# A streaming encoder layer: two blocks of expert look-ups as one dense sweep, the other look-ups in one lane

## The reference

```
h   = x @ w_in                       # q, k, v of 8 forgetting heads (64 wide) and 4 differential heads (2x64), 8 gates
A   = softmax(q k^T / 8 + D[t] - D[s], causal) @ v          # D: running sum of log gates
B   = (softmax(q1 k1^T / 8 + bias) - lam * softmax(q2 k2^T / 8 + bias)) @ v    # chunk-causal, then RMS norm
x   = LayerNorm(alpha * x + concat(A, B) @ w_out)
q   = x @ w_pq                       # 8 heads x 2 halves x 128
s   = q . sub_keys                   # 128 keys in each half; top 16 of each; top 16 of the 256 sums
idx = i1 * 128 + i2                  # 8 x 16 = 128 experts of 16384 for each frame
g   = softmax(top sums)
y   = sum over the 128 of  g * gelu(x . u_tab[idx]) * v_tab[idx]
x   = LayerNorm(alpha * x + y)
```

## Time and profile before

| | us |
|---|---|
| median of three runs | 2214.57 |
| span of the profiled execution | 2113.0 |
| whole time of the profiled execution | not shown; the runs lie between 2211.59 and 2216.9 |
| PE, DVE, ACT, POOL busy | 1847.5, 1189.1, 694.1, 1293.6 |
| bytes moved by DMA | 759.05 MB, mean 359 GB/s |

### The profile page before, as it was taken

One profiled execution on the slowest core, in us unless ns is written; L12 is line 12 of the kernel. 1 busy time (PEld: TensorE's weight loads), 2 busy tenths in 40 slices (PEclk: granted clock), 3 DMA queues, 4 the chain that ended last, 5 costly groups with the idle time before them and its releaser, 6 DMA issues.

```text
span 2113.0 us, 25770 instructions
## 1 busy us (share of the span) xinstructions
PE 1847.5 (87%) x7056; PEld 1048.4 (50%) x7056; DVE 1189.1 (56%) x2936; ACT 694.1 (33%) x1925; POOL 1293.6 (61%) x1198
## 2 busy tenths in 40 slices
PE   6795999999879999998798999987999998986776
PEld 5564544446445444455464454553655554552332
DVE  2349444557864445478645354787434454797543
ACT  1301324632222246322222464222245663222221
POOL 2004774766667756666577566666446675667774
PEclk9897999999989999999899999999999999998989
DMA  9457999999999999999999999999979999999996
GB/s 344 170 183 287 408 408 383 339 360 399 404 347 399 408 391 330 360 392 399 345 400 408 392 328 360 390 400 347 368 287 353 373 398 387 345 366 344 396 408 264
DMA packets 213316, 759.05 MB, mean 359 GB/s; under 512 B 24400, under 2 KB 28792, under 8 KB 212904
## 3 DMA queue, kind: packets, MB, share of 16 engines
q0 software_dynamic: 167168, 612.07, 75.6%
q1 hardware_dynamic: 45992, 145.17, 18.1%
HBM read 747.14 MB, written 13.28 MB: 360 GB/s over the span
## 4 chain that ended last, share of the span: by engine, by line
PE 60%; DMA 17%; DVE 10%; issue 6%; ACT 4%; POOL 3%; DVEq 0%; POOLq 0%; ACTq 0%; SPq 0%; PEldq 0%
PE acc L629 34%; DMA vbuf<-in_peer_v,idx_cur 13%; PE ps_o L610 4%; PE ps_o L434 4%; DVE ubuf L1006 3%; PE ps_o L569 3%; PE ps_o L550 3%; PE ps_s L493 3%; DMA wring<-in_w_qk 2%; PE ps_t L513 2%; POOL ubuf L1049 2%; PE ps_o L461 2%; PE ps_s L497 1%; DMA ubuf<-in_peer_u,idx_cur 1%; ACT L675 1%
## 5 line engine op out<-in xcount | busy, mean ns | idle before, releaser
L629 PE MATMUL acc<-vbuf,diag 128*128 128x512 f32 x2304 | 1060.3, 612 | 118.1 <-DMA vbuf<-in_peer_v,idx_cur 98.6
L1049 POOL DMA_INDIRECT ubuf<-in_peer_u,idx_cur x576 | 663.3, 1152 | 394.7 <-DVE hid L1006 234.3
L629 PEld LDWEIGHTS acc<-vbuf,diag 128*128 128x128 f32 x2304 | 436.9, 196 | 673.0 <-issue 629.5
L1006 DVE CUSTOM_DVE_ANT_0 ubuf<-ubuf,x_cur 128x1024 f32<-128x1024 f32 x576 | 677.2, 1222 | 159.9 <-DMA ubuf<-in_peer_u,idx_cur 137.9
L1049 POOL DMA_INDIRECT vbuf<-in_peer_v,idx_cur x576 | 610.3, 1060 | 232.5 <-issue 154.1
L747 ACT ACTIVATE diag<-ident,coef 128x128 f32<-128x128 f32 x576 | 193.1, 392 | 153.8 <-PE acc L629 141.5
L434 PE MATMUL ps_o<-xT,wring 128*128 128x128 f32 x1280 | 170.9, 299 | 62.5 <-DMA wring<-in_w_qk 30.4
L434 PEld LDWEIGHTS ps_o<-xT,wring 128*128 128x128 f32 x1280 | 167.3, 214 | 76.8 <-issue 29.3
L832 DVE CUSTOM_DVE_ANT_0 region<-ps_s,region 128x512 f32<-128x512 f32 (+2 forms) x80 | 59.5, 744 | 235.8 <-PE ps_s L497 151.9
L610 PEld LDWEIGHTS ps_o<-region,wring 128*128 128x128 f32 x1280 | 151.3, 195 | 18.4 <-issue 16.6
L610 PE MATMUL ps_o<-region,wring 128*128 128x128 f32 x1280 | 152.7, 279 | 3.9 <-ACT region L710 3.9
(11 more groups left out here) (169 smaller groups left out, 1399.8 us busy)
## 6 DMA issues: line engine op xcount, KB each, us to landing
wring<-in_w_qk SPq DMA_DIRECT2D x80, 512.0 KB, 7.6
wring<-in_w_pq SPq DMA_DIRECT2D x80, 512.0 KB, 7.2
wring<-in_w_out SPq DMA_DIRECT2D x40, 512.0 KB, 7.2
wring<-in_w_v SPq DMA_DIRECT2D x20, 512.0 KB, 8.4
ubuf<-in_peer_u,idx_cur POOLq DMA_INDIRECT x576, 7.8
vbuf<-in_peer_v,idx_cur POOLq DMA_INDIRECT x576, 8.5
region<-scr_tpl SPq DMA_DIRECT2D x4, 1280.0 KB, 16.7
wring<-in_c_k SPq DMA_DIRECT2D x8, 512.0 KB, 7.4
```

Source lines behind the costliest of these rows:

```text
L629: last = pe.matmul(acc[:, hf * 512:(hf + 1) * 512], diag[:, j, :], vbuf[:, j, hf * 512:(hf + 1) * 512], start=first_slot, stop=last_slot)
L1006: nc.vector.tensor_tensor_reduce(out=ubuf[:, j, :], in0=ubuf[:, j, :], in1=x1_cur[:, :], scale=1.0, scalar=0.0, op0=ALU.mult, op1=ALU.add, ...
L1049: pool.indirect_dma_start(buf[:, j, :], None, a[table], bass.IndirectOffsetOnAxis(ap=idx_cur[:, at:at + 1], axis=0)).then_inc(landed_[j], 16)
```

## The change

Blocks 0 and 1 and the sample keep the gather form. Blocks 2 and 3 (256 frames) do without: a dense sweep reads both expert tables whole, 128 tiles of 128 experts. For each tile PE transposes the u tile (8 transposes), ACT copies it from PSUM, PE forms the hidden values of the 256 frames (8 matmuls with 256 columns), ACT applies Gelu, DVE multiplies with the gates of this tile, and for each four tiles PE forms the outputs (8 columns of frames' features x 4 tiles, 256 columns each), which DVE adds to `yT` in SBUF. The value part runs 24 tiles behind the hidden part.

The gates as a matrix (experts x frames) are made before: for each frame a matmul of two one-hot matrices, of the second and of the first key number, the latter scaled by the gate. POOL makes the one, DVE the other, ACT copies the result, and it is put into memory (`gate_spill`, 16 pieces of 1 MiB), from which chunks of 8 tiles are read back.

The lane of the slots (`j_`) has 320 slots: 128 of block 0, 128 of block 1, 64 of the sample, 333 steps. In a step POOL gathers u row j and v row j-9, and DVE does the dot product of slot j-3 and adds coefficient times row of slot j-12 to an accumulator in SBUF by a fused multiply and add. PE and the diagonal matrices have no part in it. The rings of rows hold four of each table.

The loop is gone: all five blocks are written out, and a function `weave` puts the steps of several lanes in one fixed order on every engine. In phase p stand beside each other: attention to queries of block p (28 steps), the projections of block p+1 (12 steps over the first 92%), the top-k of block p-1 (45 steps over the first 60%, now from a copy of the scores in SBUF), and a part of the slot lane (12 steps in phase 1, 28 in each of phases 2 to 4). Then come the gate build (64 steps) with 23 hidden steps and 20 slot steps, and the rest of the sweep (129 steps) with 217 slot steps and the sample's top-k over 5% to 40% of it.

Beside that: a prompt block takes only the keys up to its own end (128, 256, 384, 512), queries are used by halves of 64 partitions without padding, matmul results of four tiles are copied from PSUM at once, ACT instead of DVE scales most head outputs, the second norm's scale and shift are loaded spread over the partitions, the weight ring has seven places and none of the v tiles is held, and the last three norms stand at the end.

```diff
-            with pe.Fori(0, NBP - 1) as i:
-                for s, _ in enumerate(tensor_block(pe, i + 1, False)):
-                    if s >= 2:
-                        tensor_set(pe, i, s - 2)
...
+ORDER = (0, 1, 2, 3, NBP)
+SMP = ORDER.index(NBP)
+LAST = NB - 1
+DENSE = (2, 3)
+NT = len(DENSE) * P
+POS = {b: p for p, b in enumerate(ORDER)}
+WRING = 7
+X_STEPS, Y_STEPS, T_STEPS, I_STEPS = 12, 28, 45, 1
+G_STEPS = 32 * len(DENSE)
+TILES = NKEYS
+URING, VRING = 4, 8
+LAG = 24
+HRING = 30
+GTOK = 16
+TGS = NT // GTOK
+CHUNK = 8
+D_STEPS = TILES + LAG
+GRING = 4
+PARTS = ((0, POS[0]), (SLOTS, POS[1]), (2 * SLOTS, SMP))
+PSLOTS = 2 * SLOTS + DEC
+U_LAG, V_AT, V_LAG = 3, 9, 12
+J_STEPS = PSLOTS + V_LAG + 1
+J_CUTS = (0, 12, 40, 68, 96, 116, J_STEPS)
...
+X_SPAN = (0.0, 0.92)
+Y_SPAN = (0.0, 1.0)
+T_SPAN = (0.0, 0.6)
...
+        def mixers(p, y, x, t, i, j):
+            lanes = [(y(p), Y_STEPS) + Y_SPAN]
+            if p < LAST:
+                lanes.append((x(p + 1), X_STEPS) + X_SPAN)
+            if p:
+                lanes.append((t(p - 1), T_STEPS) + T_SPAN)
+                steps = range(J_CUTS[p - 1], J_CUTS[p])
+                lanes.append((j(steps), len(steps), 0.65 if p == 1 else 0.0, 1.0))
+            if p == LAST:
+                lanes.append((i(0), I_STEPS, 0.0, 0.01))
+            weave(*lanes)
+        def sweep(t, i, g, d, j):
+            weave((i(1), I_STEPS, 0.0, 1.0))
+            steps = range(J_CUTS[4], J_CUTS[5])
+            weave((g(), G_STEPS, 0.0, 1.0), (d(range(0, LAG - 1)), LAG - 1, 0.0, 1.0), (j(steps), len(steps), 0.0, 1.0))
+            steps = range(J_CUTS[5], J_CUTS[6])
+            weave((d(range(LAG - 1, D_STEPS)), D_STEPS - LAG + 1, 0.0, 1.0), (j(steps), len(steps), 0.0, 1.0),
+                  (t(LAST), T_STEPS, 0.05, 0.4))
...
+        def g_tensor(pe):
+            for n in range(G_STEPS):
+                pe.wait_ge(oh2_done, n + 1)
+                pe.wait_ge(oh1_done, n + 1)
+                if n == 0:
+                    pe.wait_ge(ids_out, len(DENSE))
+                if n >= 2:
+                    pe.wait_ge(gt_out, n - 1)
+                for j in range(4):
+                    last = pe.matmul(xb[:, n % 2, j * P:(j + 1) * P], oh2[n % 2][:, j, :], oh1[n % 2][:, j, :], start=True, stop=True)
+                last.then_inc(gt_done, 1)
+                yield
+        def d_tensor(pe, steps):
+            def turn(i):
+                pe.wait_ge(du_in[i % URING], 16 * (i // URING + 1))
+                for r in range(2):
+                    wait(pe, uT_out, 2 * i - 1 + r)
+                    for j in range(4):
+                        c = 4 * r + j
+                        last = pe.transpose(ps_s[:, c * P:(c + 1) * P], u_tile[i % URING][:, c * P:(c + 1) * P], ident[:, :])
+                    last.then_inc(uT_done, 1)
+            for i in steps:
+                if i == 0:
+                    pe.wait_ge(sc_out, 4 * NB)
+                    pe.wait_ge(qh_out, 4 * NB)
+                    pe.wait_ge(v_out, 2 * NB)
+                    turn(0)
+                if i + 1 < TILES:
+                    turn(i + 1)
+                if i < TILES:
+                    wait(pe, dg_done, i - 1)
+                    for c in range(KT):
+                        if c % 4 == 0:
+                            pe.wait_ge(uT_out, 2 * i + c // 4 + 1)
+                        last = pe.matmul(ps_o[:, i % 2, 0:NT], uT[i % 2][:, c, :], x1T[:, c, :], start=c == 0, stop=c == KT - 1)
+                    last.then_inc(dh_done, 1)
+                if i >= LAG:
+                    g, q = (i - LAG) // 4, (i - LAG) % 4
+                    if i == LAG:
+                        pe.wait_ge(gt_out, G_STEPS)
+                    if q == 0:
+                        pe.wait_ge(da_done, 4 * (g + 1))
+                        for j in range(4):
+                            v = 4 * g + j
+                            pe.wait_ge(dv_in[v % VRING], 16 * (v // VRING + 1))
+                    for dc in (2 * q, 2 * q + 1):
+                        n = KT * g + dc
+                        wait(pe, dy_out, n - 3)
+                        for j in range(4):
+                            e = 4 * g + j
+                            last = pe.matmul(y_banks[n % 4][:, 0:NT], v_tile[e % VRING][:, dc * P:(dc + 1) * P], hg[e % HRING],
+                                             start=j == 0, stop=j == 3)
+                        last.then_inc(dy_done, 1)
+                yield
...
+        def g_scalar(act):
+            for n in range(G_STEPS):
+                act.wait_ge(gt_done, n + 1)
+                tg = n // 4
+                if n % 4 == 0 and tg >= 2:
+                    act.wait_ge(spill[tg % 2], 16 * (tg // 2))
+                dst = gst[tg % 2][:, :, n % 4 * 4:n % 4 * 4 + 4].rearrange("p i t -> p t i")
+                nc.scalar.copy(dst, xb[:, n % 2, :].rearrange("p (t i) -> p t i", i=NKEYS)).then_inc(gt_out, 1)
+                yield
+        def d_scalar(act, steps):
+            def move(i):
+                if i >= 2:
+                    act.wait_ge(dh_done, i - 1)
+                for r in range(2):
+                    act.wait_ge(uT_done, 2 * i + r + 1)
+                    nc.scalar.copy(uT[i % 2][:, 4 * r:4 * r + 4, :],
+                                   ps_s[:, r * 512:(r + 1) * 512].rearrange("p (c e) -> p c e", e=P)).then_inc(uT_out, 1)
+            for i in steps:
+                if i == 0:
+                    act.wait_ge(out_k, 16 * NB)
+                    act.wait_ge(out_v, 16 * NB)
+                    move(0)
+                if i + 1 < TILES:
+                    move(i + 1)
+                if i < TILES:
+                    act.wait_ge(dh_done, i + 1)
+                    if i >= HRING:
+                        act.wait_ge(dy_done, KT * ((i - HRING) // 4 + 1))
+                    nc.scalar.activation(hg[i % HRING], ps_o[:, i % 2, 0:NT], ACT.Gelu).then_inc(dg_done, 1)
+                yield
...
+        def g_vector(dve):
+            for n in range(G_STEPS):
+                gi, k = n // 32, n % 32
+                if n == 0:
+                    dve.wait_ge(ids_out, len(DENSE))
+                    dve.wait_ge(s_iota, 1)
+                if n >= 2:
+                    dve.wait_ge(gt_done, n - 1)
+                for j in range(4):
+                    t = 4 * k + j
+                    last = nc.vector.tensor_scalar(oh1[n % 2][:, j, :], iota128[:, :], idsT[:, gi, 0, t:t + 1], idsT[:, gi, 2, t:t + 1],
+                                                   ALU.is_equal, ALU.mult)
+                last.then_inc(oh1_done, 1)
+                yield
+        def d_vector(dve, steps):
+            def gated(i):
+                c = i // CHUNK
+                if i % CHUNK == 0:
+                    dve.wait_ge(gc_in[c % 2], 16 * (c // 2 + 1))
+                dve.wait_ge(dg_done, i + 1)
+                h3 = hg[i % HRING].rearrange("p (g t) -> p g t", t=GTOK)
+                nc.vector.tensor_tensor(h3, h3, gch[c % 2][:, :, i % CHUNK, :], ALU.mult).then_inc(da_done, 1)
+            for i in steps:
+                if i == LAG:
+                    for k in range(4):
+                        gated(k)
+                if LAG <= i and i - LAG + 4 < TILES:
+                    gated(i - LAG + 4)
+                if i >= LAG:
+                    g, q = (i - LAG) // 4, (i - LAG) % 4
+                    for dc in (2 * q, 2 * q + 1):
+                        n = KT * g + dc
+                        if n == 0:
+                            dve.wait_ge(out_v, 16 * NB)
+                        dve.wait_ge(dy_done, n + 1)
+                        if g == 0:
+                            last = nc.vector.scalar_tensor_tensor(yT[:, dc, :], x1T[:, dc, :], ALPHA, y_banks[n % 4][:, 0:NT],
+                                                                  ALU.mult, ALU.add)
+                        else:
+                            dve.wait_ge(dy_out, n - KT + 1)
+                            last = nc.vector.tensor_tensor(yT[:, dc, :], yT[:, dc, :], y_banks[n % 4][:, 0:NT], ALU.add)
+                        last.then_inc(dy_out, 1)
+                yield
+        def j_vector(dve, steps, chain):
+            for j in steps:
+                k = j - U_LAG
+                if 0 <= k < PSLOTS:
+                    n = part_of(k)
+                    if k == PARTS[n][0]:
+                        dve.wait_ge(x1_done, PARTS[n][1] + 1)
+                    if k % 8 == 0 and k >= 16:
+                        dve.wait_ge(gelu_done, k // 8 - 1)
+                    dve.wait_ge(u_in[k % GRING], 16 * (k // GRING + 1))
+                    nc.vector.tensor_tensor_reduce(out=ubuf[k % GRING], in0=ubuf[k % GRING], in1=x1_part[n][:, :], scale=1.0, scalar=0.0,
+                                                   op0=ALU.mult, op1=ALU.add, accum_out=hid[:, k % 16:k % 16 + 1]).then_inc(u_used, 1)
+                k = j - U_LAG - 1
+                if 0 <= k < PSLOTS and k % 8 == 7:
```

(63 more changed lines are left out.)

1517 lines of the change are left out of this document (785 added, 732 removed).

## The result

The changed kernel takes **2727.79 us** (median of 4, 2725.32 to 2733.65), the kernel before 2215.74 beside it: ratio 1.2329 [1.2302, 1.2355]. Forecast were 2291 us and a range of 2175 to 2430. The sign was right, the size missed by 437 us, and the time lies above both slow rivals (2459 and 2498) too.

A forecast was written before the change was run, and what follows sets the result against it. PE was busy 87% and DMA nearly always, the loop 6.8% above its DMA floor. Stages, each its largest engine plus waits, summed to a 2189 us span; plus 102 around it gave 2291 us, range 2175 to 2430.

The forecast's parts named there:

- both slow rivals: Whole kernel: four-row rings starving at a full DMA, 2459 us, chance 0.15; DVE and GpSimd excluding each other, 2498, chance 0.13.
- PE gains nothing, N=256 is half of N=512: PE's total work: 1722 us before, 1737 after, with an N=256 matmul taken as 0.43 us, half of N=512.
- DVE sets the first 60% of blocks 1 to 3: Mixer stages: top-k, slots and logits on DVE set these stretches, 82 + 5, 124 + 5 and 127 + 5 us with waits.
- The weave fixes the order of each engine, so a stage costs the largest engine of that stretch, plus waits: Pricing rule for all stages; in the sweep PE sets 105 steps at 8.0 us, the lane the last 24: 982 us.
- 0.29 us is its affine select of that size: Gate build: 256 GpSimd comparisons of 128x128 at 0.29 us each, 75 us; GpSimd 150 in all, stage taken as 180.
- The range's own end from the 128x64 copy: Gate build: 0.52 us a comparison, as GpSimd's copy of 128x64, would give 133 us; the stage's ends were 158 to 240.
- Half-height queries in place of padding (columns set the time): Attention scores: queries on half the partitions without padding change nothing, since columns set the matmul's time; priced at nothing.
- around the span: Outside the profiled span: 101.6 us between the 2113.0 span and the 2214.6 timed median, kept unchanged and added.
- Exclusion of DVE and GpSimd: Rival, sweep and gate build: DVE waits while GpSimd issues gathers, +165 and +42 us, 2498 in all; chance 0.13.
- Starving four-row rings: Rival, sweep: landing of gathered rows rises from 8.5 to about 18 us at full DMA, +168, 2459 us; chance 0.15.
- Stages at their floor: Faster rival, all stages: each takes only its largest engine, span 2015, with 3% 2078, 2180 us as time; chance 0.22.
- Unrolling: Middle-block loop written out: saves three turns, at most 20 us, absent from the stages; straight code's length costs nothing.

The follow-up runs named there:

- the experiment with the tiles ahead: Changed kernel with SyncE issuing u tile i+3 in step i, ahead of the value tile's wait, instead of tile i: 2374.95 us, ratio 1.0704.
- full height: Changed kernel with the sample's queries zero-padded to 128 partitions and its decay matmul reading all 128 rows: 2675.02 us, ratio 1.2068.
- the decay rows alone: Changed kernel with only the sample's decay matmul widened from 32 to 128 partitions, queries left on 64: 2705.54 us, ratio 1.2105.
- the four edits: Changed kernel with u tiles three steps ahead, comparisons on DVE, sample at 128 partitions, top-k of blocks 2 to 4 over 85% of steps: 2166.36 us, ratio 0.977.

## Why the prediction was wrong, point by point

- **PE gains nothing, N=256 is half of N=512**: right. Eight records take 1.73 us, 0.216 each, 0.43 a matmul.
- **DVE sets the first 60% of blocks 1 to 3**: right where it was looked at. From 400 to 450 us DVE has 49.1 of 50 us with PE at 33.7, and 580 us were measured for 601.
- **"The weave fixes the order of each engine, so a stage costs the largest engine of that stretch, plus waits"**: this is the step that failed in the sweep. The sum takes in the busy time of PE, DVE, POOL and of the transfers, and leaves out the waits in SyncE's queue. That queue was priced at nothing: the prediction names the rings of the gathered rows and of the weights, and never asks in which step a u tile is issued, nor what stands ahead of it. Reading `d_sync` would have told it: the wait for `dy_done` stands ahead of the next u tile. 333 us of the miss; the experiment with the tiles ahead returns 347.
- **Gate build, "0.29 us is its affine select of that size"**: a mis-sized term, and a wait left out. The comparison is 0.60 us alone and 1.03 beside DVE's passes, 177 us in all for 75; with issues and spills GpSimd is busy 224, not 150. The range's own end from the 128x64 copy (133) was nearer. Another 58 us are the waits of the spills for ACT, behind which the next comparisons stood; the forecast has no such wait on GpSimd. It is the same omission as in the sweep, on another queue; what each of the two is worth by itself was not measured. +128, of which 122 return when DVE does the comparisons.
- **"Half-height queries in place of padding (columns set the time)", priced at nothing**: wrong in the sample. +83, of which full height returns 64, 22 of them with the decay rows alone, whose narrowing the prediction doesn't mention. Why the other 19 are missing is not shown; with the four edits the sample takes 223 for the forecast 214. The Trainium skill, "TensorE: Matmul & The Clock Gate", section "Why this matters for your kernels", says that a single matmul over 32 rows takes as long as one over 128. In this stretch a 512-column matmul over 64 or 32 rows took 2.0 us and over 128 rows 0.86, with the granted clock at 0.50 and at 1.00; the page's sentence leaves the clock out, and here the measurement decides.
- **101.6 us "around the span", kept unchanged**: wrong, and it lay the other way. They were about the distance between two levels of the kernel before (2216 and 2124 us, 92 apart). Without them the forecast is 2191 us, 1.1% under the timed 2214.6, while its span of 2189 is 3.6% above the profiled 2113: which level one compares with decides the sign. The sign came out right by luck: it comes from three faults that the forecast didn't see, and without them the sign depends on the level.
- **Exclusion of DVE and GpSimd**: refuted as it was put, for in the sweep's full steps, once repaired, DVE's passes last 1.22 and 1.29 us beside the gather issues and a step 7.84. It holds the other way round. By the Trainium skill, "SBUF — State Buffer", section "Who interferes with whom", a two-input DVE instruction contends with a GpSimd one that reads SBUF; the comparisons do read it, and they are what stretched, 0.60 to 1.03. They were not shut out for the whole of the passes: 2.49 us of passes cost four comparisons 1.73 us.
- **Starving four-row rings**: refuted. DVE waited 11.1 us in all for rows of u before its L1283 passes and 15.5 for rows of v before L1309. With the four edits and a DMA share of 0.99 in the full steps it waited 9.0 and 13.6.
- **Stages at their floor**: not met. Repaired, PE's 801 of 822 us in the full steps are its floor, but the mixers stay 568 + 223 against 721 in that rival.
- **Unrolling**: "at most 20 us" in favour of straight code. Writing out the loop alone gave 21 us at the lower level and 36 to 40 at the upper. The second half of the rule of the Trainium skill that the prediction named ("Runtime: NRT & Kernel Launch", "Instruction fetch mechanics") fits this: the program of 22157 instructions in place of 25770 came out faster at both levels. What straight code may cost inside that net gain no run separates.

Is the repaired change worth making? Against the kernel before at its usual level yes, 2 to 3%; at its lower level no, 2% slower. Against the unrolled kernel before it is 1.7% faster (2165.87 to 2203.55) or 2.9% slower (2163.34 to 2102.67). No version beats all others at both levels.

## What to carry to other kernels

Write down, for each in-order queue and the DMA-issuing engine first of all, what stands ahead of each transfer at the moment when it is needed: a ring of four tiles hides nothing when the issue of the next one waits until the consumer has emptied it. Price an instruction that the trace doesn't show at the dear end of its bounds where its engine comes near to setting the stage. And ask of a profile whether its span is that of the timed runs, before anything is added to it.

## What was not expected of the hardware

- A step down in the height of a matmul's operands can cost the clock: 0.50 with 64- and 32-row matmuls of 512 columns at PE busy 50 of 50 us, 1.00 at 128 rows (800 to 850 us).
- The issue of a u tile right behind a gate chunk (1024 KB) occupied SyncE for 3.3 to 10.5 us in 13 cases of the changed kernel's sweep, where others take 0.43.
- The kernel before, with 1152 gathers, runs at 2120 to 2130 or at 2209 to 2259 us for a whole series, with its row passes and its PE records as long at either; the four-edit kernel, with 640, took 2163 to 2167 in four series, beside either.
